# Moving 25 of 128 dot products, and the weighted sums after them, to earlier places in a two-phase expert layer

## The reference, cut to what matters

```python
expert = k1 * PEER_N_KEYS + k2
g = jax.nn.softmax(top_s.astype(jnp.float32), axis=-1).astype(hb.dtype)
ue = expert_u[expert]
act = jax.nn.gelu(jnp.einsum('td,thkd->thk', hb, ue), approximate=False) * g
ve = expert_v[expert]
return jnp.einsum('thk,thkd->td', act, ve)
```

## Time and profile before

| what | value |
|---|---|
| median of three executions | 3511.97 us |
| the profiled execution | 3512.54 us, span 3510.8 us |
| up phase (PE, beats 0 to 127) | about 656 to 1277 us |
| down phase (PE, chunks 0 to 127) | 1281.5 to about 1824 us |
| PE, DVE, ACT, POOL busy, share of the span | 97%, 63%, 42%, 18% |
| mean granted TensorE clock, share of 2.4 GHz | 0.988 |

### The profile page before, as it was taken

The page is one execution under the profiler, slowest core; times in us unless marked ns, Lnnn a source line. Parts: engine busy times, 40 slices in busy tenths (PEclk is TensorE's granted clock), DMA queues, the critical chain, the costliest instruction groups (busy, mean ns, idle before and its releaser), DMA issues.

```text
span 3510.8 us, 51343 instructions
## 1 busy us (share of the span) xinstructions
PE 3392.0 (97%) x19633; PEld 2948.8 (84%) x19633; DVE 2224.6 (63%) x4546; ACT 1473.3 (42%) x2577; POOL 641.3 (18%) x549
## 2 busy tenths in 40 slices
PE   5999999999999999999989999999999889999997
PEld 4888887999999999999987678778888766777886
DVE  6567875799896668888884552474333346446443
ACT  3233334356767643333344542362122356445223
POOL 0000000037788835443420000000000000000000
PEclk9999999999999999999999999999999899999999
DMA  7534553379989999999962012101221221211232
GB/s 274 200 119 166 200 192 114 119 243 295 294 291 340 291 323 378 364 359 378 384 251 79 31 43 73 37 19 61 67 66 55 84 78 37 87 58 47 99 96 96
DMA packets 219874, 595.84 MB, mean 170 GB/s; under 512 B 17776, under 2 KB 101360, under 8 KB 216176
## 3 DMA queue, kind: packets, MB, share of 16 engines
q1 hardware_dynamic: 159312, 405.84, 33.4%
q0 software_dynamic: 36864, 134.23, 11.1%
q10 hardware_dynamic: 23456, 52.48, 4.0%
HBM read 531.67 MB, written 60.82 MB: 169 GB/s over the span
## 4 chain that ended last, share of the span: by engine, by line
PE 91%; DVE 5%; DMA 2%; issue 1%; ACT 1%; POOL 0%; ACTq 0%; DVEq 0%
PE bank L807 66%; PE bank L1007 14%; PE bank L1133 3%; PE bank L976 2%; PE bank L1119 2%; PE bank L832 2%; DMA rows<-in_urows,rk 1%; DMA WR<-in_weights 1%; PE bank L894 0%; DVE WL L1653 0%; DVE SrowA L2247 0%; DVE X L2396 0%; PE bank L964 0%; DVE OF L2393 0%; PE bank L859 0%
## 5 line engine op out<-in xcount | busy, mean ns | idle before, releaser
L1653 DVE TENSOR_TENSOR WL<-WR,WH 128x1024 fp32r<-128x1024 f32 x512 | 628.3, 1228 | 559.4 <-ACT WH L1227 510.0
L1227 ACT ACTIVATE WH<-WR 128x1024 fp32r<-128x1024 f32 x512 | 538.2, 1059 | 579.7 <-PE bank L1007 285.2
L807 PE MATMUL bank<-H2h,WH 128*128 128x512 f32 (+2 forms) x1608 | 574.5, 357 | 6.0 <-DVE H2l L1711 6.0
L807 PE MATMUL bank<-H2h,WL 128*128 128x512 f32 (+2 forms) x1608 | 569.5, 354 | 0.0
L807 PE MATMUL bank<-H2l,WH 128*128 128x512 f32 (+2 forms) x1608 | 568.8, 354 | 0.0
L807 PE MATMUL bank<-Hh,WH 128*128 128x384 f32 (+1 forms) x1440 | 516.1, 358 | 0.3 <-DVE WL L1653 0.2
L807 PE MATMUL bank<-Hh,WL 128*128 128x384 f32 (+1 forms) x1440 | 504.3, 350 | 0.0
L807 PE MATMUL bank<-Hl,WH 128*128 128x384 f32 (+1 forms) x1440 | 504.3, 350 | 0.0
L1007 PE MATMUL bank<-ah,WH 128*128 128x384 f32 x1024 | 344.1, 336 | 9.5 <-DVE al L1711 5.3
L807 PEld LDWEIGHTS bank<-H2h,WH 128*128 128x128 f32 (+1 forms) x1608 | 304.7, 190 | 53.7 <-DVE H2l L1711 6.7
L1007 PE MATMUL bank<-ah,WL 128*128 128x384 f32 x1024 | 343.7, 336 | 0.0
(11 more groups left out here) (363 smaller groups left out, 5572.4 us busy)
## 6 DMA issues: line engine op xcount, KB each, us to landing
WR<-in_weights SPq DMA_DIRECT2D x498, 512.0 KB
WR<-in_vrows SPq DMA_DIRECT2D x128, 512.0 KB
gelu_by_expert<-geU ACTq DMA_DIRECT2D x128, 192.0 KB
gates_by_expert<-tab SPq DMA_DIRECT2D x24, 1024.0 KB
geV<-gelu_by_expert SPq DMA_DIRECT2D x32, 768.0 KB, 8.8
Gt<-gates_by_expert SPq DMA_DIRECT2D x14, 1536.0 KB
x_kept<-X ACTq DMA_DIRECT2D x2, 3072.0 KB, 9.5
X<-x_kept ACTq DMA_DIRECT2D x2, 3072.0 KB, 11.4
```

What stands on the lines that cost most here:

```text
L807: yield nc.tensor.matmul(b[0:rows, out_cols], a, r, start=n == 0, stop=n == len(pairs) - 1)
L1227: act.activation(WH[:, n % SLOTS, :, :].rearrange("p a b -> p (a b)"), WR[:, c % SLOTS, :, :].rearrange("p a b -> p (a b)"), ACT.Copy)\
L1653: v.tensor_tensor(WL[:, n % SLOTS, :, :].rearrange("p a b -> p (a b)"), WR[:, plan.splits[n] % SLOTS, :, :].rearrange("p a b -> p (a b)"), ...
```

## The change

The due times are altered. The dots become 128 over 110 beats from beat 18 (126 by the last up-phase iteration, the last two in chunk 0). The sums become 128 over 123 chunks, from chunk 5 on. The Gelu of the dots moves from ACT's chunk 13 to chunk 3, their product with the gates from DVE's chunk 14 to chunk 4. The table load and the DMA stay in chunk 13.

```diff
 def dots_by(b):
 
-    return 15 * max(0, min(b, NK) - 18) // 16 + 2 * max(0, b - NK)
+    return PICKS * max(0, min(b, NK) - 18) // (NK - 18)
 
 
 def sums_by(c):
 
-    return PICKS * max(0, c - 14) // (NK - 15)
+    return PICKS * max(0, c - 4) // (NK - 5)
@@ ACT, down phase
                 if c + 3 < NK:
                     high(S["V", c + 3])
-                if c == 13:
+                if c == 3:
                     act.wait_ge(dots_done, 1)
                     act.activation(dots, dots, ACT.Gelu).then_inc(dots_gelu, 1)
+                if c == 13:
                     sqrt_table(2)
                     for b in range(2):
                         act.wait_ge(ge_stored[b], 16 * (NK // 2))
@@ DVE, down phase
                     if dotted == PICKS:
                         dve.wait_ge(row_used, PICKS)
                         v.engine_nop().then_inc(dots_done, 1)
-                if c == 14:
+                if c == 4:
                     dve.wait_ge(dots_gelu, 1)
                     v.tensor_tensor(dots, dots, share, ALU.mult).then_inc(dve_step, k.inc(dve_step))
                     dve.wait_ge(*k.own())
```

## The result

Six executions each: 3523.12 us median (3518.18 to 3528.65) for the changed kernel, 3510.72 (3507.22 to 3516.01) for the one before. The ratio is 1.0033, with a 95% interval of 1.0023 to 1.0043: slower by 12 us. The profiled execution took 3521.4 us, its span is 3519.7.

What follows compares the result with a forecast made beforehand. PE, busy 97% of the span, was taken as the bound. Profiled 3512.54 + 12.8 (up phase: 6.05 + 1.7 + 3.3 + 1.7) - 7.7 (down phase) = 3517.6, predicted as 3517 us, range 3500 to 3530.

Steps and rivals of the forecast that it cites:

- the signs that I had named for being right: PE idle 2 to 4 us at groups 21 and 53, beat 127 later by 10 to 13, 360 matmuls in 65 us.
- Down phase: Chunks 0 to 14: of 10.15 us lost, 7.7 go as 25 dots leave chunks 0 to 13.
- The step that gave the fall at the seam to the seam: Where the phases meet: 4.19 us idle at 1281.53 and its clock fall of 2.4 us stay without the dots.
- The costs set at 0 for the earlier Gelu and the thinner sums: Down phase: Gelu in chunk 3, product in chunk 4 and sums at 1.04 a chunk each cost 0.
- POOL in the first block: Up phase: POOL's late `hotB` makes PE 6.05 us late at group 21, then 6.7 us two groups on.
- POOL in the second block: Up phase, group 53: the run of long `hotB` comes again with a lead of 0.1 and costs 3.3 us.
- From beat 86: Late up phase, from 1053 us: DVE is busy only six tenths, which covers the 10 extra dots, so 0.
- The clock: Up phase, groups 21 and 53: idle of 3.7 us each makes the clock fall, 1.7 us each; bounds 0 and 6.8.
- Rival A: Up phase: only DVE's delays reach PE, 3.3 us, and POOL catches up; 3508 us; chance 0.22.
- B: Faster: the seam at 1281.53 closes with the early chunks empty and the up phase holds; 3498 us; chance 0.13.
- C: Slower: four row buffers run short, DVE waits for rows in iterations 43 to 49, 9.2 us more; 3526 us; chance 0.15.
- D: Down phase: a Gelu wait at chunk 4 or late rows for sums lose the 7.7 us gain; 3525 us; chance 0.05.

Runs made afterwards that it cites:

- the dots alone: The kernel before with only the dots' due times changed to the new pace, Gelu and sums as before: 3524.35 us, up phase 641.9, down phase 534.6.
- POOL relieved: The changed kernel with POOL building two quarters of `hotB` instead of three and TensorE reading one twice: 3505.56 us, up phase 623.8.
- both loads: The kernel before plus 24 two-input DVE pieces and 24 POOL comparisons over beats 19 to 127, no more rows gathered: 3527.96 us, up phase 637.1.
- a quarter moved to DVE: The changed kernel, but from group 32 on DVE builds two quarters of `hotB` and POOL two: 3518.65 us, up phase 638.2.
- the thinner pace: The kernel before, up phase untouched, late dots at 1.25 a chunk over chunks 0 to 20, sums from 22: 3502.98 us, ratio to before 0.9975.

## Why the prediction was right or wrong

I predicted 3517 us within 3500 to 3530, and "no change" at 0.61. The time was 3523 and lay in the range; the ratio of 1.0033 is just past the bound of 0.3%, in a case to which I had given 0.24. The path was the forecast's (PE late at the hot gates behind a POOL without room); its largest term, the up phase, was put at 12.8 us and came to 19.9. Of the signs that I had named for being right, the 360 matmuls are there (64.8 us for 65). The late groups are not the ones named: 17, 18, 20 and 50 with 1.75 to 2.06 us of idle time, none over 0.3 at group 21 and 0.75 at group 53. And beat 127 ends 19 us later, not 10 to 13.

**Down phase.** I took 7.7 us as gone; 7.8 went. (By the two formulas it is 24 dots that leave it, not 25: 102 are done before it in the kernel before and 126 in the changed one. And the lead of one dot begins at iteration 19, not 21.) Leaving the dots out altogether gives 7.4, moving them alone 7.9. The step that gave the fall at the seam to the seam and not to the dots is borne out: 4.35 and 4.32 us idle, the same 6.8 us at half clock. The costs set at 0 for the earlier Gelu and the thinner sums hold, the up phase and down phase of the dots alone being those of the change within 0.6 us.

**POOL in the first block.** I had one jump at group 21 and 6.7 us in all. The stops over 0.3 us up to group 22 add up to 9.3 us at hot gates and 0.4 at a low half, 9.0 more than before, and they begin at group 5, not 18. What failed is the way POOL's time was carried over. I shifted its old timeline by DVE's delay and added only the one extra gather of iteration 43. But POOL's work grew longer as it lost its waits: 157 instead of 131 `hotB` begin beside a two-input instruction, their mean rose from 984 to 1148 ns, that of a gather from 1206 to 1322. A sum of the work in one beat at the old durations (three at 0.984, 1.16 at 1.206 and the idle time before a gather, 4.6 of 5.05 us) would still have left room; it takes the durations that POOL has when it doesn't wait (4.98 us, above) to see that there is none.

**POOL in the second block.** Forecast 3.3 us; the stops grew by 4.8 (1.46, 2.23, 0.74 and 0.92 against 0.57).

**From beat 86.** I put 0, because DVE is busy only six tenths there. 1.4 us of stops came (groups 83 and 84). It was the wrong engine to look at: POOL was busy 85% of the time from 1060 to 1240 us before, and at the pace of 1.55 dots a beat the same beats cost more than 10 us, all at hot gates.

**The clock.** I took two falls of 1.7 us; there were two, of 3.4 us each at 0.50, so 1.7 apiece. That the total fits is partly luck: they came behind two stops with 2.0 and 2.1 us of idle time, at groups 20 and 50, not behind idle times of 3.7 us at groups 21 and 53. Together: 9.0 + 4.8 + 1.4 + 3.4 = 18.6 of the 19.9; the other 1.3 is in delays below 0.3 us each.

**Rival A** (DVE's delays only, 3.3 us) describes a kernel that I then ran: with POOL relieved the up phase costs 2.4. It was out by what it left out. **B** fell: the seam does not close, with late dots or without. **C**, the row ring, was seen at its edge: 14.5 us of waits in the changed kernel, 67.9 when gathers come a beat later. At the change's pace it was not needed for a loss of this size: both loads without any more rows give 15.7 us beside 16.5. **D** is excluded by the down phase.

**The rule that I weighed.** The Trainium skill (GPSIMD Engine Reference, Specifications) says that VectorE instructions with two SBUF inputs are in contention with GpSimd. The traces agree: `hotB` of 590 to 638 ns where they meet no such instruction and 1421 ns on the mean where they begin beside one, and in the added pieces 777 to 787 ns against 591 to 607 beside a reduction. With this rule I put the sum about 2.4 us higher, at 3520 us, for one dot in each block. That was too narrow a use of it. The instructions with two inputs were there already, and what changed is how much of them `hotB` meets: 53.9 us more, with 47.3 us more for `hotB`. How much of the 19.9 us of up phase comes from this and how much from the 22 more gathers, no run parts. Nor do the records say why 11 of the 131 took less than 650 ns all the same.

## What to carry to other kernels

Before work is moved into a phase, add up for each engine that has to deliver something in every beat what one beat asks of it, its issuing of DMAs included, and compare it with the beat's length: an engine that shows waits and a low share over the span can be full in that stretch, and what hid its long instructions was its waiting. Take durations from stretches in which the engine doesn't wait, and look at what the engine beside it runs: here VectorE's instructions with two SBUF inputs stopped GpSimd's, and a wait that kept the two apart was worth something. A releaser in a row of the timeline is to be checked against the other inputs' last records; here the one named had been done for 5 us. And where a resource was overrun at two items a step, try to thin the items in place first: here the thinner pace had all of the gain and none of the cost.

## What the hardware showed that I had not expected

The 24 additional POOL instructions and the 24 additional pieces on DVE cost 8.0 and 7.6 us, and 15.7 together: they add up although both reach PE through the same `hotB`. Idle times of 2.02 and 2.06 us had a fall of the granted clock to 0.50 (1.2 GHz) for 3.4 us behind them in the changed kernel. The 2.00 us at its group 17 had none, and the same 2.00 us in the run with a quarter moved to DVE had one; in the run with both loads 1.86 and 1.85 us had none. So near 2 us the idle time alone doesn't tell whether the clock falls. And the same 128x128 comparison on POOL lasts from 0.59 to 3.4 us, by whether DVE runs instructions with two SBUF inputs beside it; the indirect DMA's own instruction on POOL goes the same way, 992 ns on the mean where it meets none and 1314 where it begins beside one, before the change.
